# Layer 0 of a hybrid decoder trunk: six gate units from plain float32 to three float32r passes

## The reference, cut to what matters

```python
for i in range(DEPTH):                                   # DEPTH = 2, x is 256 x 1024
    z = x @ w_in[i]                                      # 1024 x 3328
    q, k, v, u, g_attn, g_ssm = jnp.split(z, splits, axis=-1)
    a_out = sliding_window_attention(q, k, v, attn_sinks[i], rel_bias)
    s_out = s5_mixer(u, ...)                             # diagonal complex state space, GELU, GLU (w_glu)
    merged = (jax.nn.sigmoid(g_attn) * (a_out @ w_branch_attn[i])
              + jax.nn.sigmoid(g_ssm) * (s_out @ w_branch_ssm[i]))
    x = layer_norm(DEEPNORM_ALPHA * x + merged @ w_out[i], ln1_g[i], ln1_b[i])
    ffn = swiglu(...) if i % 2 == 0 else moe_swiglu(...)
    ple = jax.nn.sigmoid(x @ ple_w_gate[i]) * (p[i] @ ple_w_proj[i])
    x = layer_norm(DEEPNORM_ALPHA * x + ffn + ple, ln2_g[i], ln2_b[i])
```

## Time and profile before

| | us |
|---|---|
| median of 3 runs | 1608.61 (1607.15 to 1608.81) |
| the profiled execution | 1610.91 |
| its span (first to last instruction) | 1608.9 |
| TensorE busy | 1575.2 (98%) |
| VectorE busy | 1347.0 (84%) |
| ScalarE busy | 983.8 (61%) |
| GpSimd busy | 163.8 (10%) |
| mean granted TensorE clock | 0.994 of full speed |

### The profile page before, as it was taken

The page is one execution under the profiler, slowest core; times in us unless marked ns, Lnnn a source line. Parts: engine busy times, 40 slices in busy tenths (PEclk is TensorE's granted clock), DMA queues, the critical chain, the costliest instruction groups (busy, mean ns, idle before and its releaser), DMA issues.

```text
span 1608.9 us, 23927 instructions
## 1 busy us (share of the span) xinstructions
PE 1575.2 (98%) x8964; PEld 1336.6 (83%) x8964; DVE 1347.0 (84%) x1295; ACT 983.8 (61%) x892; POOL 163.8 (10%) x173
## 2 busy tenths in 40 slices
PE   9999999999999999999999999999999999999996
PEld 7889799999899978888888888888888888888884
DVE  8876856655687788999998999998999998999998
ACT  5324444334546437776777777777677777767763
POOL 5000139950300000000000000000000000000000
PEclk9999999999999999999999999999999999999998
DMA  9334855554444567999999999999999998999993
GB/s 290 125 118 143 300 175 193 188 182 131 131 132 147 199 230 292 366 369 358 361 369 331 354 368 369 353 371 336 350 365 357 359 374 333 357 361 367 364 356 124
DMA packets 169446, 456.53 MB, mean 284 GB/s; under 512 B 7638, under 2 KB 60919, under 8 KB 168872
## 3 DMA queue, kind: packets, MB, share of 16 engines
q1 hardware_dynamic: 168472, 450.87, 78.0%
q0 software_dynamic: 768, 4.75, 0.8%
q10 hardware_dynamic: 144, 0.05, 0.0%
HBM read 453.02 MB, written 2.62 MB: 283 GB/s over the span
## 4 chain that ended last, share of the span: by engine, by line
PE 86%; DVE 9%; issue 3%; DMA 1%; ACT 1%; DVEq 0%; ACTq 0%; POOL 0%; POOLq 0%
PE psum L729 20%; PE psum L731 19%; PE psum L730 19%; PE psum L736 5%; PE psum L737 5%; PE psum L738 5%; PE psum L836 5%; DVE wl L462 2%; PE psum L1194 1%; PE psum L861 1%; PE psum L798 1%; DMA ring<-in_w_out 1%; DVE hid L2182 1%; ACT wh L456 1%; DVE small L1787 1%
## 5 line engine op out<-in xcount | busy, mean ns | idle before, releaser
L462 DVE TENSOR_TENSOR wl<-ring,wh 128x2048 fp32r<-128x2048 f32 x269 | 609.5, 2288 | 67.3 <-ACT wh L456 63.5
L456 ACT ACTIVATE wh<-ring 128x2048 fp32r<-128x2048 f32 x307 | 581.5, 1919 | 126.3 <-PE psum L731 78.6
L730 PE MATMUL psum<-wl,xgh 128*128 128x512 f32 x896 | 349.1, 390 | 0.0
L729 PE MATMUL psum<-wh,xgh 128*128 128x512 f32 x704 | 282.0, 401 | 1.4 <-DVE wl L462 0.8
L731 PE MATMUL psum<-wh,xgl 128*128 128x512 f32 x704 | 274.9, 391 | 0.0
L730 PEld LDWEIGHTS psum<-wl,xgh 128*128 128x128 f32 x896 | 168.5, 188 | 32.4
L729 PE MATMUL psum<-wh,hidh 128*128 128x512 f32 x440 | 172.7, 393 | 3.7 <-DVE wl L462 2.9
L730 PE MATMUL psum<-wl,hidh 128*128 128x512 f32 x448 | 174.4, 389 | 0.0
L731 PE MATMUL psum<-wh,hidl 128*128 128x512 f32 x440 | 171.4, 390 | 0.0
L462 DVE TENSOR_TENSOR wl<-ring,wh_spare 128x2048 fp32r<-128x2048 f32 x72 | 164.6, 2287 | 3.0 <-ACT wh_spare L456 3.0
L729 PEld LDWEIGHTS psum<-wh,xgh 128*128 128x128 f32 x704 | 132.2, 188 | 34.1 <-DVE wl L462 6.0
(11 more groups left out here) (425 smaller groups left out, 2722.9 us busy)
## 6 DMA issues: line engine op xcount, KB each, us to landing
ring<-in_moe_gu SPq DMA_DIRECT2D x224, 1024.0 KB, 7.1
ring<-in_moe_dn SPq DMA_DIRECT2D x112, 1024.0 KB, 7.2
ring<-in_w_in SPq DMA_DIRECT2D x25, 1024.0 KB, 5.3
ring<-in_w_gu SPq DMA_DIRECT2D x22, 1024.0 KB, 5.0
ring<-in_w_dn SPq DMA_DIRECT2D x11, 1024.0 KB, 5.0
ring<-in_w_out SPq DMA_DIRECT2D x8, 1024.0 KB, 6.8
ring<-in_w_pg SPq DMA_DIRECT2D x8, 1024.0 KB, 5.4
ring<-in_w_ba SPq DMA_DIRECT2D x4, 1024.0 KB, 5.0
```

The lines of the kernel that those rows point to most:

```text
L456: eng.activation(parts(u)[0], ring[:, ring_slot(u), :], ACT.Copy).then_inc(hi_ready, 1)
L462: eng.tensor_tensor(lo, ring[:, ring_slot(u), :], hi.bitcast(F32), ALU.subtract).then_inc(lo_ready, 1)
L729: pe.matmul(dst, ah, bh, start=first, stop=False, skip_group_check=True)
L730: pe.matmul(dst, ah, bl, start=False, stop=False, skip_group_check=True)
```

## The change

Layer 0's units from 7 on are split (`FIRST_SPLIT = 7`), so units 7 to 11 and 13 go from plain to three passes. Their high parts are made by ScalarE between its other steps; the low parts of units 7 and 8 by GpSimd, those of 9, 10, 11 and 13 by VectorE. For this the input is split too: `x0h` (ScalarE, in the place of `xa`) and `xIl` (VectorE). The load of x into `xa` moves behind that of unit 17. With it: GpSimd's shifts of layer 0 go to ScalarE, ahead of its copies of the bias rows; the bias products go between the products of units 1 and 2; VectorE's first output powers go ahead of its first scan; the transposes of the values go ahead of the local products.

```diff
-PLAIN_UNITS = 13
+FIRST_SPLIT = 7
+PLAIN_UNITS = FIRST_SPLIT
...
-HI_PLACE = ({i: p for i, p in LATE_HI.items() if i != 13}, EARLY_HI | LATE_HI)
+HI_PLACE = ({i: p for i, p in (EARLY_HI | LATE_HI).items() if i >= FIRST_SPLIT}, EARLY_HI | LATE_HI)
...
+        x0h = place("x0h", [P, KD, SEQ], F32R, at=xa_at)
...
-            return l == 1 or i == 12 or i >= 14
+            return l == 1 or i >= FIRST_SPLIT
...
+                    if u == 18:
+                        split_used(sp, 13)
                         sp.dma_start(xa[:], x.rearrange("(b p) d -> p b d", p=P)).then_inc(x_dma, 16)
...
                     u, g = state["u"], state["g"]
-                    if l:
+                    split = is_split(*of_layer(u))
+                    if split:
+                        if l == 0:
+                            pe.wait_ge(x0_lo, 1)
                         pe.wait_ge(lo_ready, split_index(u) + 1)
...
-                            if l:
-                                mm = product_by_column(dst, xTh[:, k, :], xIl[:, k, :], u, KD, k, t * P, k == 0, k == KD - 1)
+                            if u in (1, 2) and k % 4 == 2:
+                                bias_row_of(4 * (u - 1) + 2 * t + k // 4)
+                            if split:
+                                mm = product_by_column(dst, (xTh if l else x0h)[:, k, :], xIl[:, k, :], u, KD, k, t * P, k == 0, k == KD - 1)
...
-                project("u")
-                if l == 0:
-                    bias_rows(0)
-                project("u")
-                if l == 0:
-                    bias_rows(1)
+                project("u"), project("u")
...
-                    local_products(0), input_states(0), turn_values(), scores(0)
+                    turn_values(), local_products(0), input_states(0), scores(0)
...
-                    if l == 0:
-                        copy_rows(g)
                     early_hi(3 + g)
...
-                    shift_inputs(lambda d, s: act.activation(d, s, ACT.Copy), g, (0, 1), shifted_ready[0])
+                    shift_inputs(lambda d, s: act.activation(d, s, ACT.Copy), g, (0, 1) if l else range(4), shifted_ready[0])
+                    if l == 0:
+                        copy_rows(g)
...
                     copy_maps(0)
+                    act.activation(x0h[:], xT[:], ACT.Copy).then_inc(x0_hi, 1)
...
             pool.wait_ge(decay_ready, 1)
+            pool.wait_ge(x0_lo, 1)
+            for i in range(FIRST_SPLIT, 9):
+                make_lo(pool, i)
+                pool.wait_ge(lo_ready, split_index(i) + 1)
             for l in range(DEPTH):
-                for g in range(2):
+                for g in range(2) if l else ():
...
+                    output_powers(dve, link, 0, (scratch_a[:, 0:512], scratch_b[:, 0:512]), 8, (0,))
+                    dve.wait_ge(x0_hi, 1)
+                    dve.tensor_tensor(xIl[:], xT[:], x0h[:].bitcast(F32), ALU.subtract).then_inc(x0_lo, 1)
                     scan_states(0), logits(0)
-                    output_powers(dve, link, 0, temps, 8, (0,))
                     normalise(0), scan_states(1)
```

More of the change, by code:

```diff
@@ L113, in program @@
         ringr = place("ring_split", [P, RING, UNIT], F32R, at=0)
+        xa_at = top[0]
         xa = place("xa", [P, NB, D])
@@ L290, in program @@
         angle_dma, table_dma, xT_dma = sem("state_parameters_landed"), sem("bias_tables_landed"), sem("transposed_input_landed")
+        x0_hi, x0_lo = sem("input_hi_ready"), sem("input_lo_ready")
         warmed = sem("blank_products_done")
@@ L391, in is_split @@
         def is_split(l, i):
-            return l == 1 or i == 12 or i >= 14
+            return l == 1 or i >= FIRST_SPLIT
         def split_index(u):
-            return u - PLAIN_UNITS if u >= 14 else 0
+            return u - PLAIN_UNITS
         def split_used(eng, u, laps=0):
@@ L446, in hi_free @@
                 eng.wait_ge(xs_ready, 2 * l + 2)
-            elif l and where == "norm":
-                split_used(eng, LAYER_UNITS + 13)
+            elif where == "norm":
+                split_used(eng, l * LAYER_UNITS + 13)
             elif l:
@@ L744, in open_group, with bias_row_of @@
                 return bank[g % 2]
-            def bias_rows(turn):
-                if turn == 0:
+            def bias_row_of(h):
+                if h == 0:
                     pe.wait_ge(table_dma, 32)
[L750 to L755, removed]
+                if h >= 4:
+                    pe.wait_ge(bias_row, h - 3)
+                pe.matmul(bank[bias_banks[h % 4]][:, 0:BIAS_W], relb_sb[0:BUCKETS + 1, h, :], hot_sb[0:BUCKETS + 1, :],
+                          start=True, stop=True).then_inc(bias_ps, 1)
             def turn_maps(l):
@@ L853, in input_states @@
                     pe.wait_ge(gin_ready, 8 * (l + 1))
-                    for s in shifted_ready:
-                        pe.wait_ge(s, n + 1)
+                    pe.wait_ge(shifted_ready[0], n + 1)
+                    if l:
+                        pe.wait_ge(shifted_ready[1], b + 1)
                     if b:
@@ L1674, in _ @@
             pool.wait_ge(decay_ready, 1)
+            pool.wait_ge(x0_lo, 1)
+            for i in range(FIRST_SPLIT, 9):
+                make_lo(pool, i)
+                pool.wait_ge(lo_ready, split_index(i) + 1)
             for l in range(DEPTH):
-                for g in range(2):
+                for g in range(2) if l else ():
                     pool.wait_ge(u_ready, 2 * l + g + 1)
-                    pool.wait_ge(*((shifted_zeroed, 2), (zeroed, 3))[l])
+                    pool.wait_ge(zeroed, 3)
                     shift_inputs(pool.tensor_copy, g, (2, 3), shifted_ready[1])
@@ L2001, in _ @@
                     scan_states(0), early_lo(5), logits(0), early_lo(6), normalise(0), early_lo(7), scan_states(1, 8)
+                if l == 0:
+                    dve.wait_ge(lo_ready, split_index(9))
                 attended_lo(0), early_lo(9), logits(1), gelu_in_half(0), normalise(1), early_lo(10)
```

## The result

| | before | changed |
|---|---|---|
| median of the runs, us | 1608.71 (1607.15 to 1611.01, 6 runs) | 1619.77 (1615.79 to 1623.73, 6 runs) |
| profiled execution: time, span, mean clock | 1610.91, 1608.9, 0.994 | 1615.79, 1614.0, 0.992 |

The ratio is 1.0063, with a 95% interval of 1.005 to 1.0077: the change costs 8 to 12 us, 11.1 by the medians. I had forecast 5.4 and a range that ended at 1617.0. Slower was right, the size was not. One thing stands out before any row is read: the profiled execution is the fastest of the six, its span only 5.1 us longer than before, and the six lie 8 us apart where those of before lay 4. So there are two questions: whether the 5.1 us are those that I had worked out, and where the others lose 1 to 8 us more.

The account below looks back on a forecast made before the run. TensorE bound the kernel, but VectorE's chain was equally long before the first output states. Terms +8.0 there, -3.3 to the GLU, -0.3 behind it, +1.0 clock gave +5.4 on 1608.61: 1614.0 us, range 1605.5 to 1617.0.

Parts of the forecast that it names:

- wait for unit 1: TensorE, before unit 1's products: waits from 13.9 to 16.04 us until unit 1 has landed.
- bias rows inside units 1 and 2: TensorE up to the maps' transposes: unit 1 starts 0.6 us earlier and carries 2.8 us more, +2.1 us.
- values ahead: TensorE behind the kv unit: value transposes wait 2.1 us for ScalarE's copy, first input states come 2.4 us later.
- output powers moved: VectorE's chain: 5.5 us of powers leave the wait for exponentials, 3.4 us of waiting is uncovered, -2.1 us.
- GpSimd stops VectorE: VectorE's scan: GpSimd's two low parts stop it for 1.4 and 4.8 us, together +6.3 us.
- VectorE's chain ends: VectorE, before the first output states: chain ends at 104.7 us, putting their start at 104.8 instead of 96.80.
- output states to GLU: TensorE from the first output states to the GLU: 26.2 us instead of 29.5, -3.3 us.
- unit 15's low part: Behind the GLU: unit 13 is 1.3 us shorter, but branch products need unit 15's low part; net -0.3 us.
- clock: TensorE behind the kv unit's new wait: a possible half-speed stretch, taken as +1.0 us out of 0 to 1.7.
- a rival with a chance of 0.10: The 5 us wait before the probabilities lowers unit 7's clock; with 1.7 behind kv, +7.5, 1616.1 us; chance 0.10.
- Rivals 1 and 2: 1: GpSimd does not stop VectorE, 1607.7 us, chance 0.22. 2: also clock up in both places, 1604.9, chance 0.10.
- rival 4: Reordered places cost nothing because unit 1 lands earlier: the +2.1 goes, 1611.9 us; no chance given.

Follow-up runs that it names:

- second profile: Changed kernel run once more, nothing edited: 1619.2 us, ratio 1.0051; its profiled execution had a span of 1620.5 us.
- The run without the passes: Changed kernel with bias products in two blocks again, units 7 and 8 plain, no low parts on GpSimd: 1606.0 us, ratio 0.9977.
- short fills: Changed kernel with 4, 4 and 11 blank products in TensorE's three new waits (unit 1, values, probabilities): 1618.09 us.
- the run with the blocks: Changed kernel with the bias products in two blocks of four again, behind units 0 and 1: 1613.09 us, ratio 1.0021.

## Why the prediction was wrong

Its steps, against the profiled execution and the runs:

| step | forecast | shown |
|---|---|---|
| wait for unit 1 | 13.9 to 16.04 | to 16.34 (2.21 us) |
| bias rows inside units 1 and 2 | +2.1 | +3.3 in the first profile; **+4.9 at equal clock**; +7.7 in the second profile |
| values ahead | +2.4 | +2.5 (scan start +5.82 in all) |
| output powers moved | -2.1 | -2.1 |
| GpSimd stops VectorE | 1.4 and 4.8 | 1.08 and 4.34 |
| VectorE's chain ends | 104.7 | 104.99 |
| output states start | 104.8 | 106.03, unit 7 at 0.50 |
| output states to GLU | 26.2 us | 26.1 us |
| unit 15's low part | -0.3 net | 0.72 of waiting, -0.4 net |
| clock | +1.0, behind kv | nothing behind kv; 1.0 behind the probabilities (in 106.03) |
| span | +5.4 | +5.1 |
| median | +5.4 | +11.1, +9.4, +7.5 in the three sets of runs of the changed kernel |

**The step that failed is the first part's cost**, in its two halves. The sentence "Unit 1 starts 0.6 us earlier and carries 2.8 us more: +2.1 us" took a row between wide products for as long as one among rows, and the wide products for as long as in an unbroken unit; the mixing cost another 2.5 us. And "I take that loss as unchanged; between 0 and 1.8 us could come back" bounded the clock on one side only. The loss of 1.8 us did come back, in the profiled execution; it hid 1.6 of the 2.8 us that I had missed. In the second profiled execution it was larger than before, 4.4 us instead of 1.8: the clock was at 0.50 for 10.2 us instead of 3.4. That the low clock could last longer, with mixed products inside it, was in no bound. The run with this part alone, 6.2 us for a term of 2.1, shows it.

**The clock was under-sized for a second reason.** I put 1.0 us on the wait behind kv. In the profiles with this wait unfilled the clock fell behind it in one only (57.7 in the run with unit 1's wait filled), but after the wait for the probabilities in every profile that has it, for 6.8 us mostly (3.4 to 10.2). I knew that wait's size, 5 us, and gave its effect on the clock to a rival with a chance of 0.10; here it came in all seven such profiles, and it costs some 2.4 us on TensorE (0.9 in L921, 1.5 in unit 7), of which 1.0 shows at the output states. This wait was never filled by itself, so its share of the median is not shown.

**What was right**: all three waits with place and size, both stops of VectorE with the very steps, the transfer of the bound from TensorE to VectorE, and the reason for slower, that the change makes six units cheaper where TensorE waits anyway. The run without the passes shows that reason, by 4.8 us at the output states; the median fell by 7.1. Rivals 1 and 2, that GpSimd does not stop VectorE, are excluded by L1904 and L1919; rival 4, that the reordering costs nothing, by the maps at 45.46.

That the profiled execution agrees with the forecast to 0.3 us is partly chance: 2.8 us too little on the interleaving stand against a clock that was kind at unit 1 (1.6 us) and 0.9 us too much on the stops, and the 1.0 us of clock came in another place than I had put it.

Left open: where the clock falls in the executions without a profile (the later stages take part, by the second profile), what splits executions of the same mean clock (1615.8 and 1616.5 against 1618.5 and 1619.1 at 0.992), and whether each execution with short fills had the stall that its profile shows.

## What to carry to other kernels

A wait of 2 us on TensorE is not priced at 2 us: ask what clock the work behind it gets, and give that a bound on both sides, in the unit that will run slowly. Before an operation goes to GpSimd, look at which operands VectorE's steps have at that moment: beside VectorE's steps with an operand in PSUM it cost nothing here, and beside a step on two SBUF operands it cost what was left of its length (4.3 of 4.8 to 4.9 us), and an empty slot of VectorE itself may be the better place. Where executions lie far apart, compare their mean clocks before comparing a single profile; the first one may be the lucky one.

## What was not expected

Narrow products mixed with wide ones cost TensorE more than the two apart: 2.76 us for one row of 33 partitions and 384 columns with eight wide products, 2.47 apart, 0.3 us for each mix, at full clock. The runs do not show why. And TensorE can stand for 3.19 us in the middle of a run of small products, with a load of instructions recorded inside the gap. It came with 19 more products ahead of it in the program, and in none of the other profiles was the gap there over 0.4 us. That the load of instructions was the cause is not shown, and the other profiles speak against a load as the whole reason: in the changed kernel one is recorded at 107.0, 1.0 us behind the start of the output states, in the run with the blocks at 103.1, 2.8 us behind it, and TensorE has no gap over 0.3 us there in either.
